# The one-hot products of the gate matrix in f32r, with the gate weight in two parts

## Chip, core and metric

The kernel runs on one NeuronCore of a Trainium2 chip. The metric is the device time of one execution in microseconds (us). One execution was also recorded by the hardware profiler; times inside the kernel come from that record. Engines are named as the profile names them: PE is the matrix engine's products, PEld its weight loads, DVE the vector engine, ACT the scalar engine, POOL the GpSimd engine, SP the queue that issues most transfers.

## What is computed

Two transformer-like blocks over 256 tokens of width 2048. The change touches the last part of the second block, the retrieval over 16384 experts (`peer`): each token has 8 heads with 16 chosen experts, each with a weight g, and an expert is a pair of keys (i1, i2) out of 128 by 128.

```python
sc, pos = lax.top_k(cand, PEER_TOPK)
idx = jnp.take_along_axis(cand_idx, pos, axis=-1)      # i1 * 128 + i2
g = jax.nn.softmax(sc, axis=-1)
act = jax.nn.gelu(jnp.einsum('thkd,td->thk', u[ib], tb), approximate=False)
return jnp.einsum('thk,thkd->td', gb * act, v[ib])
```

The kernel doesn't gather rows of u and v. It multiplies all experts by all tokens, and weighs the result with a gate matrix that holds, for each token, the 128 by 128 table of summed weights (zero for an expert that was not chosen).

## The kernel before

All weights come as one stream of 128-column blocks, each 1 MB (`raw`). ACT casts each half of a block to f32r (`whi`, L337) and DVE subtracts that from the raw values to get the remainder (`wlo`, L343). PE then makes three f32r products in place of one fp32 product (high by high, high by low, low by high). f32r is a second 4-byte format of PE, into which the high part is rounded.

The stage of the change is the up-projection: 128 blocks, one for 128 experts (`product_wide`, L375 and L376). Per block there are 16 pairs of f32r products: one of 512 columns (high weights by both parts of the activations) and one of 256 columns. Block n's result is copied and added by ACT (L1775) and DVE (`usum`, L1508), and DVE prepares the remainders of block n + 2. Every engine runs a fixed program in order; semaphores tie them together. The loops over `n` in the code give the order.

The gate matrix is made beside this stage, in 64 groups of 4 tokens. `groups_at(n)` spreads them over n = 58 to 113: one group per block, and two in each seventh or so. The parts are:

- routing on DVE up to block 54, then the three tables of chosen key 1, key 2 and weight are turned by PE so that the 128 chosen entries lie on the partitions, and copied to `chosenT` (L1464);
- for group g, at DVE's step n (after `usum`), one instruction makes four one-hot tables of key 2 (`one2`, L1471, 128 by 512), and four instructions make the one-hot table of key 1 times the weight (`one1`, L1477, 128 by 128 each);
- at PE's step n + 2, after the block's products, `gate_group` (L963) multiplies the two tables for each of the 4 tokens: weights `one2`, moving operand `one1`, 128 columns, fp32;
- ACT copies the bank to `gstage` (L1757), and POOL's queue stores it.

The tables have four buffers each; DVE's group g waits for PE's group g - 4. PE's group waits for `onehots` and for ACT's copy of four groups before. The down-projection (L994 to L996) follows: per block 24 f32r products of 512 columns.

Of the kernel before, what the change touches and what calls it, by code (L numbers as in the profile page):

```python
# [13 lines left out]
T = 256  # L14
# [133 lines left out]
def build(nc, stream, xt, vecs, sgu_wt, sgu_b, relb, buckets, keys, inv_cnt, lnf, out):  # L148
    f32, f32r, u32 = mybir.dt.float32, mybir.dt.float32r, mybir.dt.uint32
    ALU, ACT, AX = mybir.AluOpType, mybir.ActivationFunctionType, mybir.AxisListType  # L150
# [7 lines left out]
    def at(name, shape, offset, dtype=f32):  # L158
        return nc.alloc_sbuf_tensor_at(name, shape, dtype, offset=int(offset))

    def ar(name, shape, kb, dtype=f32):

        return at(name, shape, ARENA + kb * KB, dtype)
# [5 lines left out]
    iota = at("iota", [128, 128], origin + 3 * KB)  # L169
# [96 lines left out]
    chosen = [ar(f"chosen{i}", [128, KC, TOPK], 26 + i) for i in range(3)]  # L266
    gsum = ar("gsum", [128, KC], 106)
    chosenT = [ar(f"chosenT{i}", [128, T], 29 + i) for i in range(3)]
    one1 = [ar(f"one1_{i}", [128, 4, 128], 16 + 2 * i) for i in range(4)]
    one2 = [ar(f"one2_{i}", [128, 4, 128], 96 + 2 * i) for i in range(4)]  # L270
    gstage = [ar(f"gstage{i}", [128, SLICES, 32, 16], 64 - 16 * i) for i in range(2)]
    gslice = [ar(f"gslice{i}", [128, T, 16], 48 + 16 * i) for i in range(2)]

# [12 lines left out]
    def bank(i):  # L286
        return pb[i]

    es = ExitStack()
    with es:  # L290
# [3 lines left out]
        def sem(name):  # L294
            if name not in made:
                made[name] = es.enter_context(nc.semaphore(name))
            return made[name]

        def vcol(name, i=0, p0=0, p1=128):
            return vec[p0:p1, VCOL[name] + i:VCOL[name] + i + 1]  # L300
# [418 lines left out]
        def _(pe):  # L719
            pe.wait_ge(sem("onehot_loaded"), 32)  # L720
            nc.tensor.matmul(bank(7)[0:16, 0:128], relb_sb[:, :], onehot_b[:, :], start=True,
                             stop=True).then_inc(sem("band_product"), 1)
# [9 lines left out]
            for j in range(NT):  # L732
                ins = nc.tensor.transpose(bank(4 + 3 * j)[:, 0:128], ckv[:, 1, 128 * j:128 * j + 128], ident[:, :])
# [32 lines left out]
            for r in range(4):  # L766
                for h in range(2):
                    for j in range(NT):
                        ins = nc.tensor.transpose(bank(4 + r)[:, 256 * h + 128 * j:256 * h + 128 * j + 128],
                                                  bv[:, 2 * r + h, 128 * j:128 * j + 128], ident[:, :])  # L770
# [3 lines left out]
            for r in range(4):  # L774
                pe.wait_ge(sem("vtok_ready"), r + 1)
                for h in range(2):
                    for j in range(NT):
                        hh = 2 * r + h
                        ins = nc.tensor.matmul(bank(4 + r)[:, 256 * h + 128 * j:256 * h + 128 * j + 128],
                                               vtok[:, j, 128 * hh:128 * hh + 128], sguw[:, hh, :],  # L780
                                               start=True, stop=True)
# [6 lines left out]
            for i in range(WC):  # L788

                o = bank(4 + i // 2)[:, T * (i % 2):T * (i % 2) + T]  # L790
                for k in range(2):
# [3 lines left out]
                    ins = nc.tensor.matmul(o, wlo[b.half][:, w, :], mixhi[:, r, :], start=False, stop=k == 1)  # L795
# [39 lines left out]
            for i, src in enumerate((cum, dtfs)):  # L835
                for j in range(NT):
                    ins = nc.tensor.transpose(bank(6)[:, 256 * i + 128 * j:256 * i + 128 * j + 128],
                                              src[:, 128 * j:128 * j + 128], ident[:, :])
# [15 lines left out]
            for g in range(2):  # L854
                B, C, o = xconv[:, 8 + g, :], xconv[:, 10 + g, :], bank(4 + g)
                nc.tensor.matmul(o[:, 0:256], B[:, 0:128], C, start=True, stop=True)
                nc.tensor.matmul(o[:, 256:384], B[:, 128:256], C[:, 128:256], start=True,
                                 stop=True).then_inc(sem("cb_product"), 1)
# [10 lines left out]
            for h in range(HEADS):  # L869
                if h % 2 == 0:  # L870
                    beside_ssd(3 + h // 2, 4 + h // 2)
                if h >= 2:
                    pe.wait_ge(sem("ssd_out"), h - 1)
                pe.wait_ge(sem("ssd_mat"), h + 1)
                c, m, o = h // 2, dec[h % 2], bank(6 + h % 2)
                nc.tensor.matmul(o[:, 0:256], xtok[:, 0, 128 * c:128 * c + 128], m[:, 0:256], start=True, stop=False)
                nc.tensor.matmul(o[:, 128:256], xtok[:, 1, 128 * c:128 * c + 128], m[:, 256:384], start=False,
                                 stop=True).then_inc(sem("ssd_y"), 1)
# [46 lines left out]
            for n in range(8):  # L925
# [3 lines left out]
                for i in range(4):  # L929
                    hs = 4 * q + i  # L930
                    ins = nc.tensor.matmul(bank(4 + n % 4)[:, 128 * i:128 * i + 128], pq[:, hs, 128 * j:128 * j + 128],
                                           pk[:, hs, :], start=True, stop=True)
# [24 lines left out]
            def gate_group(g):  # L957

                pe.wait_ge(sem("onehots"), g + 1)
                if g >= 4:  # L960
                    pe.wait_ge(sem("stage_full"), g - 3)
                for t in range(4):
                    ins = nc.tensor.matmul(bank(4 + g % 4)[:, 128 * t:128 * t + 128], one2[g % 4][:, t, :],  # L963
                                           one1[g % 4][:, t, :], start=True, stop=True)
                ins.then_inc(sem("gate_product"), 1)

            for n in range(CHUNKS):
# [41 lines left out]
        def _(dve):  # L1009
            st = Steps(dve, sem("dve_steps"))  # L1010
# [100 lines left out]
            for r in range(4):  # L1111
                dve.wait_ge(sem("b_spatial"), r + 1)
                t = bsq[:, 2 * r:2 * r + 2, :]
                for h in range(2):
                    bias_h = sgub[:, 2 * r + h, :].rearrange("p (a n) -> p a n", a=1).to_broadcast([128, NT, 128])
                    ins = nc.vector.tensor_tensor(bsq[:, 2 * r + h, :].rearrange("p (j n) -> p j n", j=NT),
                                                  bank(4 + r)[:, T * h:T * h + T].rearrange("p (j n) -> p j n", j=NT),
                                                  bias_h, ALU.add)
# [18 lines left out]
            for g, src in enumerate((win_a[:, 0:2, PAD:], win_b[:, 0:2, PAD:], win_a[:, 4:6, PAD:],  # L1137
                                     win_b[:, 4:6, PAD:])):
                by = cnt[:, g, :].rearrange("p (a n) -> p a n", a=1).to_broadcast([128, 2, T])
                ins = nc.vector.tensor_tensor(src, src, by, ALU.mult)  # L1140
# [58 lines left out]
            for q in range(4):  # L1199
                part = zsum[:, 4 * q:4 * q + 4, :]  # L1200
# [6 lines left out]
            for c in range(KC):  # L1207
                dve.wait_ge(sem("x1_scaled"), c + 1)
                ins = nc.vector.tensor_scalar(x1[:, c, :], zsum[:, c, :], vcol("ln_b", c), None, ALU.add)
# [19 lines left out]
            def rms_split(name, src, r, gain, n, dhi, dlo, tmp, j0=0, c0=0):  # L1229

                for c in range(n):
# [11 lines left out]
            ins = nc.vector.tensor_scalar(y[:, :], bank(b.bank)[:, 0:T], vcol("dtf_bias"), vcol("dtf_sign"), ALU.add,  # L1243
                                          ALU.mult)
# [47 lines left out]
            for r in range(4):  # L1292
                dve.wait_ge(sem("xs_turned"), r + 1)
                for h in range(2):
                    c = 2 * r + h
                    ins = nc.vector.tensor_tensor(
                        xtok[:, :, 128 * c:128 * c + 128].rearrange("p j (a d) -> p j a d", a=2),
                        bank(4 + r)[:, 256 * h:256 * h + 256].rearrange("p (j a d) -> p j a d", j=NT, a=2),
                        dtT[:, :, 2 * c:2 * c + 2].rearrange("p j (a d) -> p j a d", d=1).to_broadcast([128, NT, 2, 64]),
                        ALU.mult)  # L1300
# [159 lines left out]
            def turned_chosen():  # L1460

                dve.wait_ge(sem("chosen_turned"), 1)
                for i in range(3):
                    st.link(nc.vector.tensor_copy(chosenT[i][:, :], bank(4 + i)[:, 0:T]))  # L1464

            def onehots(g):

                o = g % 4
                if g >= 4:
                    dve.wait_ge(sem("gate_product"), g - 3)  # L1470
                nc.vector.tensor_tensor(  # L1471
                    one2[o][:, :, :], iota[:, :].rearrange("p (a n) -> p a n", a=1).to_broadcast([128, 4, 128]),
                    chosenT[1][:, 4 * g:4 * g + 4].rearrange("p (a n) -> p a n", n=1).to_broadcast([128, 4, 128]),
                    ALU.is_equal)
                for t in range(4):
                    tok = slice(4 * g + t, 4 * g + t + 1)
                    ins = nc.vector.tensor_scalar(one1[o][:, t, :], iota[:, :], chosenT[0][:, tok],  # L1477
                                                  chosenT[2][:, tok], ALU.is_equal, ALU.mult)
                ins.then_inc(sem("onehots"), 1)

            def gate(j):
# [49 lines left out]
            for t in range(NT):  # L1531
                for q in range(4):
                    dve.wait_ge(sem("rows_done"), 4 * t + q + 1)
                    part = x1tok[:, t, 512 * q:512 * q + 512]
# [12 lines left out]
                for q in range(4):  # L1547
                    part = x1tok[:, t, 512 * q:512 * q + 512]
# [350 lines left out]
```

## Time and profile before

| what | value |
|---|---|
| median of 3 runs | 3460.86 us (3460.77 to 3461.58) |
| the profiled execution, its own time | 3458.67 us |
| span from its first to its last instruction | 3456.9 us |
| PE busy | 3286.3 us, 95% of the span |
| DVE busy | 2072.9 us, 60% |
| ACT busy | 1516.0 us, 44% |
| chain that ended last | PE 89%, DVE 6%, ACT 2% |
| L963, the one-hot products, in that chain | 1% |

The page divides the span by engine and by line of the code. PE's busy time there has modelled ends, and its products overlap, so the pace of PE is read from the distance between starts and not from a product's own duration. The chain that ended last tells which instructions the end of the kernel depended on.

### The profile page before, as it was taken

The numbers are of one execution on the slowest core, as the hardware profiler recorded it, in microseconds if no ns is written. First come the engines' busy times: TensorE is split into PE (matmuls) and PEld (weight loads), VectorE is DVE, ScalarE is ACT, GpSimd is POOL, SyncE is SP. The second block draws the span as 40 slices with busy tenths as digits, with TensorE's granted clock in tenths as the row PEclk, the third lists the DMA queues.
The fourth block names the chain that finished last, engine by engine and source line by source line (L and its number), as shares of the span: only waits on it lengthen the run. The fifth ranks groups of instructions, "written<-read, shape, count | busy, mean of one in ns | idle before, by whom it ended". The sixth has DMA issues, their size and how long they took to land.

```text
span 3456.9 us, 54474 instructions
## 1 busy us (share of the span) xinstructions
PE 3286.3 (95%) x21910; PEld 3041.9 (88%) x21910; DVE 2072.9 (60%) x3174; ACT 1516.0 (44%) x2095; POOL 29.1 (1%) x44
## 2 busy tenths in 40 slices
PE   7989998999999997999888999999999999999998
PEld 7878998999999997999778988888888888888886
DVE  4446977555545446675335478967676566666665
ACT  4444434444444334434224444454444444444444
POOL 0000000000000000000000000000000000000000
PEclk9989999999999998999889999999999999999999
DMA  9323543555555542434123466656666866666663
GB/s 282 125 96 138 186 163 134 177 182 182 182 182 182 194 171 83 173 126 155 61 85 135 160 206 207 210 201 228 221 215 230 310 244 243 242 240 241 240 219 139
DMA packets 108255, 638.72 MB, mean 185 GB/s; under 512 B 11616, under 2 KB 28160, under 8 KB 38960
## 3 DMA queue, kind: packets, MB, share of 16 engines
q1 hardware_dynamic: 100368, 591.44, 48.3%
q0 software_dynamic: 7472, 44.57, 3.6%
q8 instruction: 125, 2.05, 0.2%
q14 instruction: 50, 0.41, 0.0%
q10 hardware_dynamic: 240, 0.25, 0.0%
HBM read 597.42 MB, written 38.80 MB: 184 GB/s over the span
## 4 chain that ended last, share of the span: by engine, by line
PE 89%; DVE 6%; ACT 2%; issue 1%; DMA 1%; DVEq 0%; ACTq 0%; SPq 0%
PE bank L375 14%; PE bank L358 14%; PE bank L360 14%; PE bank L359 14%; PE bank L376 7%; PE bank L994 7%; PE bank L995 7%; PE bank L996 7%; DVE wlo L343 2%; PE bank L963 2%; PE bank L497 1%; ACT whi L337 1%; PE bank L494 1%; DMA raw<-stream 1%; PE bank L508 1%
## 5 line engine op out<-in xcount | busy, mean ns | idle before, releaser
L343 DVE TENSOR_TENSOR wlo<-raw,whi 128x1024 fp32r<-128x1024 f32 x1056 | 1288.6, 1225 | 1208.5 <-ACT whi L337 1205.5
L337 ACT CAST whi<-raw 128x1024 fp32r<-128x1024 f32 x1056 | 1104.5, 1048 | 1308.8 <-PE bank L360 783.8
L358 PE MATMUL bank<-xboth,whi 128*128 128x256 f32 x3312 | 948.9, 287 | 39.9 <-DVE xboth L1225 24.1
L359 PE MATMUL bank<-xboth,whi 128*128 128x256 f32 x3312 | 942.0, 284 | 0.0
L360 PE MATMUL bank<-xboth,wlo 128*128 128x256 f32 x3312 | 941.8, 284 | 0.0
L375 PE MATMUL bank<-xboth,whi 128*128 128x512 f32 x2048 | 727.0, 399 | 0.0
L358 PEld LDWEIGHTS bank<-xboth,whi 128*128 128x128 f32 x3312 | 641.6, 194 | 42.7 <-issue 39.7
L359 PEld LDWEIGHTS bank<-xboth,whi 128*128 128x128 f32 x3312 | 641.1, 194 | 0.7
L360 PEld LDWEIGHTS bank<-xboth,wlo 128*128 128x128 f32 x3312 | 640.7, 193 | 0.0
L376 PE MATMUL bank<-xboth,wlo 128*128 128x256 f32 x2048 | 573.1, 280 | 0.0
L375 PEld LDWEIGHTS bank<-xboth,whi 128*128 128x128 f32 x2048 | 384.7, 188 | 89.8
L994 PE MATMUL bank<-whi,aghi 128*128 128x512 f32 x1024 | 398.4, 389 | 0.0
L996 PE MATMUL bank<-wlo,aghi 128*128 128x512 f32 x1024 | 398.3, 389 | 0.0
L995 PE MATMUL bank<-whi,aglo 128*128 128x512 f32 x1024 | 398.3, 389 | 0.0
L376 PEld LDWEIGHTS bank<-xboth,wlo 128*128 128x128 f32 x2048 | 386.6, 189 | 0.0
L996 PEld LDWEIGHTS bank<-wlo,aghi 128*128 128x128 f32 x1024 | 192.3, 188 | 39.9
L994 PEld LDWEIGHTS bank<-whi,aghi 128*128 128x128 f32 x1024 | 192.3, 188 | 39.9
L995 PEld LDWEIGHTS bank<-whi,aglo 128*128 128x128 f32 x1024 | 192.3, 188 | 39.8
L1767 ACT CAST aghi<-agf 128x256 fp32r<-128x256 f32 x128 | 52.1, 407 | 272.5 <-DVE agf L1491 272.5
L358 PE MATMUL bank<-mhi,whi 128*128 128x256 f32 x512 | 151.5, 296 | 12.0 <-DVE mlo L1360 6.8
L359 PE MATMUL bank<-mlo,whi 128*128 128x256 f32 x512 | 147.0, 287 | 0.0
L360 PE MATMUL bank<-mhi,wlo 128*128 128x256 f32 x512 | 147.0, 287 | 0.0
(348 smaller groups left out, 3030.8 us busy)
## 6 DMA issues: line engine op xcount, KB each, us to landing
raw<-stream SPq DMA_DIRECT2D x528, 1024.0 KB, 4.8
up_activations<-ust SPq DMA_DIRECT2D x128, 128.0 KB, 5.1
gate_matrix<-gstage POOLq DMA_DIRECT2D x8, 2048.0 KB, 14.0
gslice<-gate_matrix POOLq DMA_DIRECT2D x8, 2048.0 KB, 10.7
uin<-up_activations SPq DMA_DIRECT2D x32, 512.0 KB, 5.6
relative_band<-cband POOLq DMA_DIRECT2D x1, 3072.0 KB, 36.8
xraw<-xt SPq DMA_DIRECT2D x1, 2048.0 KB, 7.8
cbias<-relative_band POOLq DMA_DIRECT2D x1, 2048.0 KB, 20.8
```

The source lines that it names most:

```text
L337: nc.scalar.copy(whi[b.half][:, k, :], raw[b.raw][:, k, :]).then_inc(hi_done, 1)
L343: nc.vector.tensor_tensor(wlo[b.half][:, k, :], raw[b.raw][:, k, :], whi[b.half][:, k, :].bitcast(f32), ALU.subtract).then_inc(lo_done, 1)
L358: nc.tensor.matmul(o, whi[b.half][:, k, :], rhi[:, r, :], start=i == 0, stop=False)
L359: nc.tensor.matmul(o, whi[b.half][:, k, :], rlo[:, r, :], start=False, stop=False)
L360: ins = nc.tensor.matmul(o, wlo[b.half][:, k, :], rhi[:, r, :], start=False, stop=i == len(ks) - 1)
L375: nc.tensor.matmul(o[:, :], whi[b.half][:, k, :], xboth[:, :, k, :], start=k == 0, stop=False)
L376: ins = nc.tensor.matmul(o[:, 0:T], wlo[b.half][:, k, :], xhi[:, k, :], start=False, stop=k == KC - 1)
L963: ins = nc.tensor.matmul(bank(4 + g % 4)[:, 128 * t:128 * t + 128], one2[g % 4][:, t, :], one1[g % 4][:, t, :], start=True, stop=True)
L994: nc.tensor.matmul(o[:, :], a_hi[:, tok], v_hi[:, col], start=j == 0, stop=False)
L995: nc.tensor.matmul(o[:, :], a_lo[:, tok], v_hi[:, col], start=False, stop=False)
L996: ins = nc.tensor.matmul(o[:, :], a_hi[:, tok], v_lo[:, col], start=False, stop=j == CHUNKS - 1)
L1767: nc.scalar.copy(aghi[j % 3][:, :], agf[j % 3][:, :]).then_inc(sem("ag_hi"), 1)
```

## The change

The weight's column is split once into an f32r part and the remainder (two DVE instructions of 128 by 256). Each one-hot table of key 1 is made twice, times the one and times the other part, both in f32r; the table of key 2 is written in f32r as well. Each fp32 product becomes two f32r products that add into the same place.

```diff
-    one1 = [ar(f"one1_{i}", [128, 4, 128], 16 + 2 * i) for i in range(4)]
-    one2 = [ar(f"one2_{i}", [128, 4, 128], 96 + 2 * i) for i in range(4)]
+    one1 = [[ar(f"one1_{part}{i}", [128, 4, 128], at_kb + 2 * i, f32r) for i in range(4)]
+            for part, at_kb in (("hi", 16), ("lo", 8))]
+    one2 = [ar(f"one2_{i}", [128, 4, 128], 96 + 2 * i, f32r) for i in range(4)]
+    wgt_hi = ar("wgt_hi", [128, T], 104, f32r)
+    wgt_lo = ar("wgt_lo", [128, T], 105)
...
                 for t in range(4):
-                    ins = nc.tensor.matmul(bank(4 + g % 4)[:, 128 * t:128 * t + 128], one2[g % 4][:, t, :],
-                                           one1[g % 4][:, t, :], start=True, stop=True)
+                    for part in range(2):
+                        ins = nc.tensor.matmul(bank(4 + g % 4)[:, 128 * t:128 * t + 128], one2[g % 4][:, t, :],
+                                               one1[part][g % 4][:, t, :], start=part == 0, stop=part == 1)
...
                     st.link(nc.vector.tensor_copy(chosenT[i][:, :], bank(4 + i)[:, 0:T]))
+                st.link(nc.vector.tensor_copy(wgt_hi[:, :], chosenT[2][:, :]))
+                st.link(nc.vector.tensor_tensor(wgt_lo[:, :], chosenT[2][:, :], wgt_hi[:, :].bitcast(f32),
+                                                ALU.subtract))
...
                 for t in range(4):
                     tok = slice(4 * g + t, 4 * g + t + 1)
-                    ins = nc.vector.tensor_scalar(one1[o][:, t, :], iota[:, :], chosenT[0][:, tok],
-                                                  chosenT[2][:, tok], ALU.is_equal, ALU.mult)
+                    for part, weight in enumerate((wgt_hi[:, :].bitcast(f32), wgt_lo)):
+                        ins = nc.vector.tensor_scalar(one1[part][o][:, t, :], iota[:, :], chosenT[0][:, tok],
+                                                      weight[:, tok], ALU.is_equal, ALU.mult)
```

On PE, at the end of the first block with groups (n = 60), this stood between the block's last products and the next block's first; an fp32 product is one row here, `x4` stands for four in a row:

```order
L375 MATMUL bank<-xboth,whi_57 128x512
L376 MATMUL bank<-xboth,wlo_59 128x256
L963 MATMUL bank<-one_0_182,one_0_186 128x128 x4
L963 MATMUL bank<-one_1_183,one_1_187 128x128 x4
L375 MATMUL bank<-xboth,whi_58 128x512
L376 MATMUL bank<-xboth,wlo_60 128x256
```

In the changed program the first of the two groups begins so; eight rows of L967 make a group, the high and the low table in turn (three lines of code were added above, so L375 is L378, L376 is L379 and L963 is L967; `one_hi` and `one_lo` are the two tables of key 1, `one_0` that of key 2):

```order
L378 MATMUL bank<-xboth,whi_57 128x512
L379 MATMUL bank<-xboth,wlo_59 128x256
L967 MATMUL bank<-one_hi_182,one_0_190 128x128
L967 MATMUL bank<-one_lo_186,one_0_190 128x128
L967 MATMUL bank<-one_hi_182,one_0_190 128x128
```

Each product of a group has become a product with the high and one with the low table, at the same place between the blocks.

On DVE, at n = 58, the work of two groups stood before the remainders of the next block:

```order
L1508 TENSOR_TENSOR usum_197<-bank,upart_195 128x256
L1471 TENSOR_TENSOR one_0_186<-iota,chosenT_180 128x512
L1477 TENSOR_SCALAR one_0_182<-iota,chosenT_179,chosenT_181 128x128 x4
L1471 TENSOR_TENSOR one_1_187<-iota,chosenT_180 128x512
L1477 TENSOR_SCALAR one_1_183<-iota,chosenT_179,chosenT_181 128x128 x4
L343 TENSOR_TENSOR wlo_60<-raw_54,whi_58 128x1024 x2
```

In the changed program (L343 is L346, L1508 is L1516, L1471 is L1478, L1477 is L1485) the first of the two groups begins so, with eight rows of L1485:

```order
L1516 TENSOR_TENSOR usum_203<-bank,upart_201 128x256
L1478 TENSOR_TENSOR one_0_190<-iota,chosenT_180 128x512
L1485 TENSOR_SCALAR one_hi_182<-iota,chosenT_179,wgt_hi 128x128
L1485 TENSOR_SCALAR one_lo_186<-iota,chosenT_179,wgt_lo 128x128
L1485 TENSOR_SCALAR one_hi_182<-iota,chosenT_179,wgt_hi 128x128
```

The second group ends so, and the next block's remainders follow:

```order
L1485 TENSOR_SCALAR one_hi_183<-iota,chosenT_179,wgt_hi 128x128
L1485 TENSOR_SCALAR one_lo_187<-iota,chosenT_179,wgt_lo 128x128
L346 TENSOR_TENSOR wlo_60<-raw_54,whi_58 128x1024 x2
L1516 TENSOR_TENSOR usum_204<-bank,upart_202 128x256
L1478 TENSOR_TENSOR one_2_192<-iota,chosenT_180 128x512
```

Four instructions of 128 by 128 per group have become eight, all of them ahead of the next remainders; the table of key 2 is still one instruction. Once, after the copies to `chosenT`, a cast to `wgt_hi` and a subtraction to `wgt_lo` have been added. Nothing else moves on any engine.

## Rows read from the trace of the kernel before

**Rows 1.** the page: the chain that ended last, share of the span by engine

```profile
PE 89%; DVE 6%; ACT 2%; issue 1%; DMA 1%; DVEq 0%; ACTq 0%; SPq 0%
```

**Rows 2.** the chain from 2300 to 2700 us: shares, then pieces (start us, us)

```profile
by line: PE bank L375 56.9%; PE bank L376 28.9%; PE bank L963 14.3%
...
2329.57 0.89 PE bank L963 x8
2336.01 0.89 PE bank L963 x8
2342.55 0.89 PE bank L963 x8
```

**Rows 3.** timeline of PE and PEld at two groups (start us, us, engine, line)

```profile
2500.37 1.87 PEld L963 LDWEIGHTS bank<-one,one 128*128 128x128 f32 x16
2500.49 1.95 PE L963 MATMUL bank<-one,one 128*128 128x128 f32 x16
...
2502.16 0.19 PEld L375 LDWEIGHTS bank<-xboth,whi 128*128 128x128 f32 x1
```

**Rows 4.** single lines, duration ns minimum/median/maximum: fp32 128, fp32 256, f32r 256 columns

```profile
L931 PE MATMUL bank<-pk,pq x64: 275/275/348, 1959.3 to 1966.4; 128*128 128x128 f32 x64
...
L409 PE MATMUL bank<-zsum,ones x32: 377/378/483, 1209.1 to 1292.7; 128*128 128x256 f32 x32
...
L358 PE MATMUL bank<-yhi,whi x512: 283/283/283, 654.2 to 1183.7; 128*128 128x256 f32 x171
```

**Rows 5.** timeline of the weight loads where f32r products start after idle time

```profile
642.53 0.19 PEld L358 LDWEIGHTS bank<-xboth,whi 128*128 128x128 f32 x1 [0.84 <-DVE wlo L343]
642.64 0.19 PEld L359 LDWEIGHTS bank<-xboth,whi 128*128 128x128 f32 x1
642.76 0.19 PEld L360 LDWEIGHTS bank<-xboth,wlo 128*128 128x128 f32 x1
```

**Rows 6.** timeline of PE in the down-projection, f32r products of 512 columns

```profile
3000.02 0.39 PE L994 MATMUL bank<-whi,aghi 128*128 128x512 f32 x1
...
3000.70 0.39 PE L994 MATMUL bank<-whi,aghi 128*128 128x512 f32 x1
```

**Rows 7.** timeline of PE in the up-projection, twice the first and last of 19 L375

```profile
2099.69 0.40 PE L375 MATMUL bank<-xboth,whi 128*128 128x512 f32 x1
...
2106.05 0.40 PE L375 MATMUL bank<-xboth,whi 128*128 128x512 f32 x1
...
2709.95 0.40 PE L375 MATMUL bank<-xboth,whi 128*128 128x512 f32 x1
...
2716.19 0.40 PE L375 MATMUL bank<-xboth,whi 128*128 128x512 f32 x1
```

**Rows 8.** DVE groups by line and form: count, busy us, mean ns

```profile
L1477 DVE TENSOR_SCALAR one<-iota,chosenT,chosenT 128x128 f32<-128x128 f32 x256 | 71.1, 342 | 0.0
...
L551 DVE TENSOR_SCALAR fprob<-fprob,fsmall 128x256 f32<-128x256 f32 x16 | 5.6, 348 | 0.0
...
L550 DVE TENSOR_SCALAR fprob<-fprob,fsmall 128x128 f32<-128x128 f32 x16 | 4.6, 286 | 0.6
```

**Rows 9.** timeline of DVE at a step with two groups, to the next remainders

```profile
2489.92 0.42 DVE L1508 TENSOR_TENSOR usum<-bank,upart 128x256 f32<-128x256 f32 x1
2490.25 0.69 DVE L1471 TENSOR_TENSOR one<-iota,chosenT 128x512 f32<-128x512 f32 x1
2490.85 1.11 DVE L1477 TENSOR_SCALAR one<-iota,chosenT,chosenT 128x128 f32<-128x128 f32 x4
2491.88 0.69 DVE L1471 TENSOR_TENSOR one<-iota,chosenT 128x512 f32<-128x512 f32 x1
...
2493.50 1.22 DVE L343 TENSOR_TENSOR wlo<-raw,whi 128x1024 fp32r<-128x1024 f32 x1
2495.22 1.23 DVE L343 TENSOR_TENSOR wlo<-raw,whi 128x1024 fp32r<-128x1024 f32 x1 [0.50 <-ACT whi L337]
```

**Rows 10.** one window: busy of PE, PEld, DVE, ACT, POOL, granted clock, DMA share

```profile
2315.00:2680.00 365.00, 365.00 (x2277) 326.25 (x2277) 252.48 (x471) 178.84 (x284) 6.25 (x7) 1.00 0.65 222
```

## The prediction

> **What bounds the kernel now.** I read the chain that ended last first: PE holds 89% of the span [rows 1]. Then the same chain in the stretch of the change: between 2300 and 2700 us it is only PE, 56.9% L375, 28.9% L376 and 14.3% L963, the one-hot products [rows 2]. So every nanosecond of L963 is a nanosecond of the kernel, and nothing that DVE, ACT or a transfer does there is late. PE is busy all 365.00 us of the window from 2315 to 2680 at a granted clock of 1.00, the 2.4 GHz level; DVE is busy 252.48 us of it [rows 10].
>
> What L963 costs comes from starts, since the durations overlap. One fp32 product is recorded as two weight loads and two products. Over two groups, sixteen records, the first weight load starts at 2500.37 and that of the next block's first product at 2502.16: 1.79 / 16 = 112 ns for each [rows 3]. The chain gives the same: 0.89 us for eight [rows 2]. All 64 groups are 512 records, 57.3 us, and 28.7 us would go if two f32r products cost half of one fp32 product.
>
> **PE: 256 fp32 products out, 512 f32r products in.** Before, there are two records for each fp32 product and each takes 112 ns; after, there are 512 f32r products with a record and a weight load each. The number of records stays at 512, so all depends on what an f32r product of 128 columns costs against 112 ns. The trace has no f32r product under 256 columns, so I bound it.
>
> By columns alone it would be cheap. fp32 products last 275 ns with 128 columns and 378 with 256: 103 ns for 128 columns, two PE cycles a column. f32r products last 283 ns with 256 columns [rows 4] and start 120 ns apart (642.64 to 642.76, which is spacing of weight loads and products alike [rows 5]), and those of 512 columns start 227 ns apart (0.68 us for three [rows 6]). That is 107 ns for 256 columns, one cycle a column, and a fixed 13. For 128 columns: 53 + 13 = 67 ns.
>
> But each product first needs its weights, and the next load begins only when the product before has begun. How long a load takes shows where PE has been idle: the first f32r load starts at 642.53 and the second at 642.64, 0.11 us later, though no product stood in the way of the first [rows 5]. The second load can only begin when the first weights have moved on, so an f32r load of 128 weights takes about 108 ns, against 67 ns of product. Under 256 columns the load is the longer of the two. The Trainium skill says so too: TensorE: Matmul & The Clock Gate, section LDWEIGHTS, has the load take P / 1.2 ns, 107 ns for 128 columns, whatever the contraction; by that the products would cost 512 x (107 - 112) = 2.6 us less than before.
>
> So the lower bound of the mechanism is 108 ns: 512 x (108 - 112) = -2.0 us. The upper one is the pace of f32r products of 256 columns, 120 ns, if the 13 ns come on top of the load: 512 x (120 - 112) = +4.1 us. I take 110, near the load, because the fp32 records that have the same load run at 112 with 107 ns of columns: 512 x (110 - 112) = **-1.0 us**.
>
> **PE: the pace of the wide products.** One pair of L375 and L376 took 6.36 / 18 = 353 ns at 2100 us and 6.24 / 18 = 347 ns at 2710 us, at the same clock and with nothing else in between [rows 7]. The groups toggle it: they follow each other 6.44 us apart and then 6.54 [rows 2], so a block differs by 0.10 us. I count two quick blocks to one slow among the 55 with groups, 37 and 18 (an estimate: the rows show one of each), and the 12 behind them as quick [rows 7]. I can't say from the rows which pace follows an f32r group. All quick would be -1.8 us, all slow 49 x 0.10 = +4.9 us. I take no change.
>
> **DVE: 256 more instructions.** L1477 lasts 342 ns, but the next starts earlier: the four and the table of key 2 take 1.63 us (2490.25 to 2491.88), the four from 2490.85 take 1.03, so 257 ns each [rows 9]. Each group gets 4 x 0.257 = 1.03 us more, 66 us in all. At one group a step this falls into idle time: DVE's load is (252.48 + 61 x 1.03) / 365 = 86% with the 61 groups of the window [rows 10]. At a step with two groups it is 2.06 us: the remainders that began at 2493.50 begin at 2495.56, the next at 2496.8 instead of 2495.22 [rows 9]. Behind them wait `usum` and the next tables, and PE for the remainders. PE reads those of 2493.50 when it starts the block behind its own two groups, at 2502.16 [rows 3], 7.4 us after they were ready (1.22 us from 2493.50). A delay of 2.1 us stays hidden and is worked off in the two steps that follow. The tables themselves are used two steps later, from 2500.37, and would be ready at 2495.56. The raw blocks are reloaded 2 us later at most, against a ring of four. What hides all of it is PE; if PE's load went away, DVE's 86% would be the next bound.
>
> The two instructions of the weight's split run once, under a microsecond, at a step without groups: hidden. ACT, POOL and the queues do the same as before.
>
> **The sum.** 3456.9 us of span, -1.0 for the records, 0 for pace and DVE: 3455.9. The profiled execution took 3458.67 us with 3456.9 of span, and the median of the runs is 2.2 above it; the change applied to the median is 3460.86 - 1.0 = 3459.9 us. The ends of this case: 3460.86 - 2.0 - 1.8 = 3457.1 and 3460.86 + 4.1 + 4.9 = 3469.9.
>
> **Rivals.**
>
> (a) The f32r product of 128 columns isn't one quick pass. Only 256 and 512 columns are seen at one cycle a column. If below that PE treats it as it treats an fp32 product, each of the 512 costs two records, 224 ns: 512 x 112 ns = +57.3 us, 3518 us. For it: every product of 128 columns in the trace runs at two cycles a column. Against: those are all fp32, and fp32 of 256 columns does too [rows 4], so it goes with the format and not with the number of columns.
>
> (b) The load doesn't bound. If the load could begin before the product ahead of it, 67 ns would stand: 512 x (67 - 112) = -23.0 us, 3437.8 us. Against: the spacing of 0.11 us of loads behind an idle PE [rows 5]. The Trainium skill (TensorE: Matmul & The Clock Gate, section Back-to-back issue gap) goes this way: it has pairs of load and product at 128 columns sustain about 81 ns. By it the sum would be 512 x (81 - 112) = -15.9 us; nothing in this trace runs at that pace, and all weights here are 4-byte.
>
> (c) DVE becomes the bound. It has 365 us for 61 groups; full load comes at (365 - 252.48) / 61 = 1.84 us more per group, so at (1.84 + 1.03) / 8 = 359 ns for each of the eight instructions, against 257 now. An f32r output at half the element rate would add 62 ns (348 ns for 256 elements, 286 for 128 [rows 8]) and give 319: still below. It decides only if the instructions stop overlapping and their duration grows as well, to 342 + 62 = 404 ns: 64 x 8 x 45 ns = 23 us, less the 7.4 us that PE has in hand, +16 us, 3476 us.
>
> (d) The change doesn't do what it says: PE would need fewer records than 512 for a gain. That is (b) by another way, for instance if the second product of a pair kept its weights. L358 and L359 have the same weights one after the other, and each has its own load [rows 5]: no such saving is made.
>
> **How the numbers follow.** About 0.2%, 6.9 us, is what a measurement of this kernel can tell from no change: 3453.9 to 3467.8. The load-bound case has a chance of 0.77, of which 0.04 lie above 3467.8 (slow records and the slow pace together). (a) 0.15, (b) and (d) 0.05, (c) 0.03. Faster 0.05, same 0.73, slower 0.15 + 0.03 + 0.04 = 0.22. The range takes the whole first case and (c) and leaves (a) and (b) out, 0.20 together: 3455 to 3477.
>
> **What would show it.** In the changed trace the product line has 512 records again. From the first load of a group to the next block's first load divided by eight is 108 to 120 ns if I am right, 67 if (b), 224 (or 1024 records) if (a). The chain between 2300 and 2700 us is still PE alone; a wait of PE for `wlo` or the tables there would be (c). The four instructions that are now eight keep a distance near 257 ns. The periods of 6.44 and 6.54 us show the pace. What would make me wrong without any of this: a change of pace beyond both of those seen, since the rows give its size but no reason.

## The result: slower by 4.8 us, all of it in the pace of the wide products

The changed kernel takes 3465.55 us (median of 20 runs), the kernel before 3460.77 us beside it: 4.8 us more, a ratio of 1.0014 with a 95% interval of 1.0007 to 1.002. The forecast was 3459.9 us. The measured time lies inside the range of 3455 to 3477 and under the 0.2% that were called no change, but it moved the other way.

The first place to look is where the time is. The two rows are the products of 512 columns of the up-projection, before and changed: duration in ns (minimum, median, maximum), then the start of the first and of the last of them.

```profile
L375 PE MATMUL bank<-xboth,whi x2048: 391/395/481, 1966.4 to 2746.0; 128*128 128x512 f32 x187
L378 PE MATMUL bank<-xboth,whi x2048: 393/398/481, 1968.5 to 2753.0; 128*128 128x512 f32 x187
```

The stage took 779.6 us before and takes 784.5 us now, 4.9 us more. The profiled executions differ by 7.1 us (3456.9 and 3464.0 us of span): the other 2.1 us lie ahead of the stage, where the two programs do the same. The stage starts at 1966.4 to 1970.8 us in the profiled executions of this study.

PE still holds the chain, with 89% of the span as in [rows 1]. Between 2300 and 2700 us the chain is again PE alone, as in [rows 2], and the one-hot products (now L967) have a smaller share of it, 13.6% against 14.3%. The pieces are those of the groups (start in us, length):

```profile
by line: PE bank L378 57.7%; PE bank L379 28.8%; PE bank L967 13.6%
...
2344.85 0.84 PE bank L967 x8
2351.39 0.84 PE bank L967 x8
2357.93 0.84 PE bank L967 x8
```

Before, the groups followed each other 6.44 us apart and then 6.54 [rows 2]. Here it is 6.54 and 6.54. The blocks behind the last group differ too. The next two rows are PE's timeline of the changed kernel, the first and the seventeenth of its products of 512 columns, so 16 pairs:

```profile
2709.91 0.40 PE L378 MATMUL bank<-xboth,whi 128*128 128x512 f32 x1
...
2715.57 0.40 PE L378 MATMUL bank<-xboth,whi 128*128 128x512 f32 x1
```

5.66 us for 16 pairs, 353 ns a pair, where [rows 7] had 347 ns in the same place. So all blocks now run at the slow pace. What hardly changed is the price of the group. These are the weight loads of one group and of the next block's first product in the changed kernel:

```profile
2491.20 0.19 PEld L967 LDWEIGHTS bank<-one_hi,one 128*128 128x128 f32 x1
2491.32 0.19 PEld L967 LDWEIGHTS bank<-one_lo,one 128*128 128x128 f32 x1
...
2492.10 0.19 PEld L378 LDWEIGHTS bank<-xboth,whi 128*128 128x128 f32 x1
```

From 2491.20 to 2492.10 there are eight loads, 0.90 / 8 = 112 ns each, the same as with fp32 in [rows 3]. The group's piece of the chain is 0.84 us where it was 0.89, because the second product of a group now starts 0.06 us behind the first (2491.32 and 2491.38) and not 0.11; the loads don't come closer for it.

And DVE, in the window of [rows 10], is busy 313.06 us in place of 252.48, with nobody waiting for it. PE has no wait in that window; DVE's own wait for ACT has shrunk from 111.2 to 51.9 us. The first row is the kernel before, the others are the changed one:

```profile
L343 DVE TENSOR_TENSOR wlo<-raw,whi 128x1024 fp32r<-128x1024 f32 x111 | 136.0, 1225 | 111.2 <-ACT whi L337 111.2
...
2315.00:2680.00 365.00, 365.00 (x2254) 324.09 (x2253) 313.06 (x725) 177.49 (x283) 6.25 (x7) 1.00 0.63 219
...
L346 DVE TENSOR_TENSOR wlo<-raw,whi 128x1024 fp32r<-128x1024 f32 x112 | 135.4, 1220 | 51.9 <-ACT whi L340 51.9
L1485 DVE TENSOR_SCALAR one_hi<-iota,chosenT,wgt_hi 128x128 fp32r<-128x128 f32 x248 | 84.3, 340 | 0.0
L1485 DVE TENSOR_SCALAR one_lo<-iota,chosenT,wgt_lo 128x128 fp32r<-128x128 f32 x248 | 84.2, 340 | 0.0
```

The starts of all blocks in the trace of the kernel before give the number of quick ones: 36 of the 55 between the first and the last group, and the 12 behind them. In the changed kernel none is quick. 48 blocks at 0.10 us each are 4.8 us, and the medians differ by 4.8.

### The profile page after: what moved, and what is told of

It reads as the page before. It is cut to its first block, busy times and chain, and to the rows that moved or that the text cites. A ratio compares the mean times of both kernels' runs of the same rounds, so it can differ in the third digit from the quotient of the medians.

```text
span 3464.0 us, 54732 instructions
## 1 busy us (share of the span) xinstructions
PE 3291.9 (95%) x21910; PEld 3043.9 (88%) x21910; DVE 2134.4 (62%) x3432; ACT 1515.8 (44%) x2095; POOL 29.3 (1%) x44
## 4 chain that ended last, share of the span: by engine, by line
PE 89%; DVE 6%; ACT 2%; issue 1%; DMA 1%; DVEq 0%; ACTq 0%; SPq 0%
PE bank L378 14%; PE bank L361 14%; PE bank L363 14%; PE bank L362 14%; PE bank L379 7%; PE bank L998 7%; PE bank L999 7%; PE bank L1000 7%; DVE wlo L346 2%; PE bank L967 2%; PE bank L500 1%; ACT whi L340 1%; PE bank L497 1%; DMA raw<-stream 1%; PE bank L511 1%
## 5 line engine op out<-in xcount | busy, mean ns | idle before, releaser
L346 DVE TENSOR_TENSOR wlo<-raw,whi 128x1024 fp32r<-128x1024 f32 x1056 | 1286.6, 1224 | 1151.8 <-ACT whi L340 1148.8
L378 PE MATMUL bank<-xboth,whi 128*128 128x512 f32 x2048 | 730.2, 400 | 0.0
L379 PE MATMUL bank<-xboth,wlo 128*128 128x256 f32 x2048 | 575.2, 281 | 0.0
L378 PEld LDWEIGHTS bank<-xboth,whi 128*128 128x128 f32 x2048 | 385.1, 188 | 92.7
L379 PEld LDWEIGHTS bank<-xboth,wlo 128*128 128x128 f32 x2048 | 387.1, 189 | 0.0
```

The costliest lines, as they stand in the source:

```text
L346: nc.vector.tensor_tensor(wlo[b.half][:, k, :], raw[b.raw][:, k, :], whi[b.half][:, k, :].bitcast(f32), ALU.subtract).then_inc(lo_done, 1)
L378: nc.tensor.matmul(o[:, :], whi[b.half][:, k, :], xboth[:, :, k, :], start=k == 0, stop=False)
L379: ins = nc.tensor.matmul(o[:, 0:T], wlo[b.half][:, k, :], xhi[:, k, :], start=False, stop=k == KC - 1)
```

## The experiments

Times are medians; each stands beside runs of the kernel before on the same chip (3460.1 to 3460.8 us in all of them). "Quick" and "slow" are the two paces of a pair of wide products, 347 and 353 ns.

### DVE's part of the change alone

```diff
+    one1lo = [ar(f"one1_lo{i}", [128, 4, 128], 8 + 2 * i, f32r) for i in range(4)]
...
+                    nc.vector.tensor_scalar(one1lo[o][:, t, :], iota[:, :], chosenT[0][:, tok],
+                                            chosenT[2][:, tok], ALU.is_equal, ALU.mult)
                     ins = nc.vector.tensor_scalar(one1[o][:, t, :], iota[:, :], chosenT[0][:, tok],
```

> The kernel before with DVE's part of the change alone: for each token a second, unused table of key 1 in f32r, so eight instructions per group in place of four; PE keeps its fp32 products. Theory P (what PE runs between the blocks sets the pace of the wide products, and DVE has nothing to do with it): time of before within 1 us, two thirds of the blocks with groups at 347 ns a pair, one third at 353, the blocks behind at 347. Rival D (the longer DVE work beside the wide products slows their reading): about 4.8 us above before, all pairs at 353 ns.

Measured: 3460.1 us against 3460.63, ratio 0.9998 (0.9988 to 1.0007). The rows are the chain at three groups, then the busy time of the window; L964 is the one-hot product here:

```profile
2332.05 0.89 PE bank L964 x8
2338.49 0.89 PE bank L964 x8
...
2345.04 0.89 PE bank L964 x8
...
2315.00:2680.00 365.00, 365.00 (x2275) 326.12 (x2275) 314.55 (x727) 178.97 (x284) 6.25 (x7) 1.00 0.64 220
```

6.44 and 6.55: the pattern of before, with DVE busy 314.55 us of 365. From the first product behind the first groups to the first behind the last group, 56 blocks on, the traces of this run and of the kernel before both have 368.10 us. DVE's work is hidden in full and doesn't touch the pace. Theory D falls. What remains is on PE.

### What an f32r product of few columns costs

```diff
-                        ins = nc.tensor.matmul(bank(4 + g % 4)[:, 128 * t:128 * t + 128], one2[g % 4][:, t, :],
-                                               one1[part][g % 4][:, t, :], start=part == 0, stop=part == 1)
+                        ins = nc.tensor.matmul(bank(4 + g % 4)[:, 128 * t:128 * t + 64], one2[g % 4][:, t, :],
+                                               one1[part][g % 4][:, t, 0:64], start=part == 0, stop=part == 1)
```

> The changed kernel with each one-hot product cut to its first 64 of 128 columns; it leaves out half of the gate matrix. Theory L (the weight load bounds a product of few columns): the eight of a group still start 112 ns apart, eight in 0.84 to 0.90 us of the chain. Rival C (the columns bound, at two cycles each): 54 ns fewer each, 58 ns apart, 27 us less in all.

Measured: 3461.78 us, one run. The weight loads of a group, then the chain at three groups:

```profile
2489.83 0.19 PEld L967 LDWEIGHTS bank<-one_hi,one 128*128 128x128 f32 x1
...
2490.61 0.19 PEld L967 LDWEIGHTS bank<-one_lo,one 128*128 128x128 f32 x1
...
2331.51 0.81 PE bank L967 x8
2338.05 0.81 PE bank L967 x8
...
2344.50 0.81 PE bank L967 x8
```

Eight loads take (2490.61 - 2489.83) / 7 = 111 ns each with half the columns. The load is the floor, as the prediction had it: the 27 us of theory C are not there. The spacing of the groups, 6.54 and 6.45, shows something that was not asked: the pace turns again. These groups are f32r throughout, as in the changed kernel, and have the same loads; only the columns differ. So f32r in the group is not by itself what keeps blocks slow.

### The high tables alone on PE

```diff
-                    for part in range(2):
-                        ins = nc.tensor.matmul(bank(4 + g % 4)[:, 128 * t:128 * t + 128], one2[g % 4][:, t, :],
-                                               one1[part][g % 4][:, t, :], start=part == 0, stop=part == 1)
+                    ins = nc.tensor.matmul(bank(4 + g % 4)[:, 128 * t:128 * t + 128], one2[g % 4][:, t, :],
+                                           one1[0][g % 4][:, t, :], start=True, stop=True)
```

> The changed kernel with PE multiplying the high tables alone; it leaves out the weight's low part, DVE still makes it. 256 records and loads of 112 ns fewer. Theory L and P: 28.7 us less for the records, and the slow pace stays (24 us below before, 28.7 below the changed kernel) or toggles (29 us below before). Rival (the time of the changed kernel comes from DVE's longer work): less than 20 us below the changed kernel.

Measured: 3434.64 us against 3460.48, ratio 0.9925 (0.991 to 0.994): 25.8 us below before, and 30.9 below the changed kernel, which was measured separately. The chain at three groups:

```profile
2336.10 0.39 PE bank L966 x4
...
2342.09 0.39 PE bank L966 x4
2348.18 0.39 PE bank L966 x4
```

The four products of a group are 0.39 us of the chain and the groups follow at 5.99 and 6.09 us: quick and slow blocks again. 256 loads at 112 ns are 28.7 us; the other 2.2 fit the 24 blocks that are quick in its trace, at 0.10 us each. Load and pace add up.

### Which product of the group matters: one fp32 product last, or first

```diff
+                    o = bank(4 + g % 4)[:, 128 * t:128 * t + 128]
+                    if t == 3:
+                        ins = nc.tensor.matmul(o, one2f[g % 4][:, :], one1f[g % 4][:, :], start=True, stop=True)
+                        continue
```

> The changed kernel with the fourth token of each group as one fp32 product, the last in the group (tables of its own in fp32, still eight small DVE instructions for key 1 and 2 together). Eight records per group as before. Theory P1 (the product right in front of a block sets the pace): the pattern of before comes back, two quick blocks to one slow, and the blocks behind are quick: the time of before within 1 us. Rival P2 (any f32r products of 128 columns in the group, or the phase in which the group is entered, keep it slow): 4.8 us above before.

The other kernel has `t == 0` in the same place.

> The same with the first token of each group as the fp32 product, f32r products last. Theory P1: slow pace after every group, 4.8 us above before. If the way into the group decides instead (the first product right behind the wide ones), the pattern and time of before.

Measured: 3465.2 us with the fp32 product last (ratio 1.0016, 1.0006 to 1.0025) and 3465.4 us with it first (1.0014, 1.0004 to 1.0024). The chain at three groups with the fp32 product last, then at two with it first; L973 is f32r, L970 fp32:

```profile
2331.15 0.62 PE bank L973 x6
2331.76 0.28 PE bank L970 x2
2337.69 0.62 PE bank L973 x6
...
2344.24 0.62 PE bank L973 x6
...
2333.30 0.62 PE bank L973 x6
...
2339.84 0.62 PE bank L973 x6
```

6.54 and 6.55 us in the first, 6.54 in the second. Both are as slow as the changed kernel, so neither the product right ahead of a block nor the one right behind it decides by its format. Theory P1 falls. What I had left was that the pace is a state, which the whole way through a group leaves or turns.

### Four or eight products thrown in where there are no groups

Blocks 8 to 56 are slow in both kernels. Here products that nobody uses were put behind blocks 12, 25 and 38 of the kernel before:

```diff
+                if n in (12, 25, 38):
+                    pe.wait_ge(sem("x1tok_out"), 8)
+                    for t in range(4):
+                        nc.tensor.matmul(bank(4)[:, 128 * t:128 * t + 128], ident[:, :], ident[:, :], start=True,
+                                         stop=True)
```

> The kernel before with four fp32 products of 128 columns into a bank that is free, after blocks 12, 25 and 38, where all blocks run slow (353 ns a pair); the products are not used. They cost 0.89 us each time. Theory S (the pace is a state that the way through a group sets and that then stays): after at least one of the three places the blocks turn to 347 ns and stay there up to the next place, 12 or 13 blocks of 5.55 us. Rival (quick blocks need something of the groups' stretch, such as ACT's and DVE's work on them): all stay at 353.

The f32r form:

```diff
+                    for t in range(8):
+                        nc.tensor.matmul(bank(4)[:, 128 * (t // 2):128 * (t // 2) + 128], xhi[:, t, 0:128],
+                                         xhi[:, t, 0:128], start=t % 2 == 0, stop=t % 2 == 1)
```

> The same with eight f32r products of 128 columns in place of the four fp32 ones, at the same three places, at the same 0.89 us. Theory S with the difference between the kernels coming from the kind of product: all blocks stay at 353 ns. If the kind doesn't matter: the same turns as with the fp32 products.

Measured, one run each: 3459.83 us with the fp32 products, 3463.41 us with the f32r ones. First the fp32 kernel: the chain's piece of the first thrown-in products, then 16 pairs behind the first place (2099.76 to 2105.30) and 16 behind the third (2239.73 to 2245.38):

```profile
2044.94 0.89 PE bank L974 x8
...
2099.76 0.39 PE L375 MATMUL bank<-xboth,whi 128*128 128x512 f32 x1
...
2105.30 0.39 PE L375 MATMUL bank<-xboth,whi 128*128 128x512 f32 x1
...
2239.73 0.40 PE L375 MATMUL bank<-xboth,whi 128*128 128x512 f32 x1
...
2245.38 0.40 PE L375 MATMUL bank<-xboth,whi 128*128 128x512 f32 x1
```

5.54 us behind the first, 5.65 behind the third. Four products of 0.89 us turned 26 blocks to the quick pace, the second place left them quick, and the third turned them back. That is the order slow, quick, quick, slow that the groups of the kernel before go through.

The two quick stretches are not the same. The rows are the products of 512 columns in three windows of this run, behind the first, the second and the third place, with their shortest, median and longest duration in ns:

```profile
L375 PE MATMUL bank<-xboth,whi x88: 392/394/395, 2065.8 to 2095.9; 128*128 128x512 f32 x88
...
L375 PE MATMUL bank<-xboth,whi x88: 391/391/391, 2139.8 to 2170.0; 128*128 128x512 f32 x88
...
L375 PE MATMUL bank<-xboth,whi x86: 395/398/403, 2214.6 to 2244.7; 128*128 128x512 f32 x86
```

The starts say it more clearly: behind the first place the pairs take 343 and 350 ns in turn, behind the second 346, 347, 347, behind the third 349, 350, 361, over and over. So there are three repeating patterns, two of 347 ns a pair and one of 353. The groups of the kernel before lead from each to the next in a fixed turn (slow, first quick, second quick, slow), 18 times over; a block's pattern depends on the pattern ahead of the group and not on the group alone.

Now the f32r kernel, 16 pairs behind the first place and 16 behind the second:

```profile
2099.84 0.39 PE L375 MATMUL bank<-xboth,whi 128*128 128x512 f32 x1
...
2105.39 0.39 PE L375 MATMUL bank<-xboth,whi 128*128 128x512 f32 x1
...
2149.83 0.40 PE L375 MATMUL bank<-xboth,whi 128*128 128x512 f32 x1
...
2155.47 0.40 PE L375 MATMUL bank<-xboth,whi 128*128 128x512 f32 x1
```

5.55 and then 5.64 us: the first turned to quick, the second back to slow, and behind the third they stayed slow. So f32r products can turn the pace as well. In the fp32 kernel the quick blocks gave back 26 x 0.10 = 2.6 us for the 3 x 0.89 = 2.7 us that the thrown-in products took, so its time is that of the kernel before; in the f32r kernel 13 blocks gave back 1.3 us there.

The f32r kernel has two more differences further on, where its program is that of the kernel before. The four blocks ahead of its first groups are quick, and its twelve blocks behind the last group are slow, where those of before are the other way round. The groups' products were fp32 in both; what differed is the pattern in which the stream came to them.

Theory S fits: the pace is a state of the stream of pairs. In these traces it lasts as long as nothing interrupts the stream, whatever ACT and DVE do beside it, and a handful of other products may turn it either way.

### Another order of the wide products

If the state belongs to the strict alternation of 512 and 256 columns, another order has none. Two of a kind together:

```diff
-                nc.tensor.matmul(o[:, :], whi[b.half][:, k, :], xboth[:, :, k, :], start=k == 0, stop=False)
-                ins = nc.tensor.matmul(o[:, 0:T], wlo[b.half][:, k, :], xhi[:, k, :], start=False, stop=k == KC - 1)
+                for step in ((low, wide) if k % 2 else (wide, low)):
+                    ins = step()
```

`wide` is the product of 512 columns and `low` that of 256.

> The kernel before with the order of the wide block's products changed: 512, 256, then 256, 512 columns and so on in turn, so that two of a kind follow each other; the same products. Theory P (the slow pace comes from the strict alternation of 512 and 256 columns, since streams of 512 or of 256 alone always run at columns plus 13 ns): all pairs at 347 ns; the 60 blocks ahead of the groups gain 0.10 us each, the 18 slow ones among them too: 8 us below before. Rival (alternation isn't the cause): no change within 1 us, or all blocks slow, 5 us above.

> The changed kernel with the same order of the wide products as in the run with that order on the kernel before. Theory P: all 128 blocks at 347 ns a pair, the same time as that run within 1 us, so that the 4.8 us of the change are gone. Rival: the changed kernel stays 4.8 us above the other with this order.

Measured: 3456.1 us on the kernel before (ratio 0.9986, 0.9977 to 0.9995) and 3454.95 us on the changed one (0.9985, 0.9976 to 0.9994). PE's timeline of the first (L376 is 512 columns, L380 is 256), then the chain at its groups (L969), then at those of the changed kernel (L973):

```profile
2099.66 0.63 PE L376 MATMUL bank<-xboth,whi 128*128 128x512 f32 x2
...
2100.36 0.63 PE L376 MATMUL bank<-xboth,whi 128*128 128x512 f32 x2
...
2101.75 0.63 PE L376 MATMUL bank<-xboth,whi 128*128 128x512 f32 x2
...
2332.83 0.89 PE bank L969 x8
2339.31 0.89 PE bank L969 x8
...
2345.79 0.89 PE bank L969 x8
...
2332.35 0.84 PE bank L973 x8
...
2338.82 0.84 PE bank L973 x8
...
2345.29 0.84 PE bank L973 x8
```

Four products every 0.70 us (2.09 / 6 = 348 ns a pair), and groups 6.48 us apart, all alike. With this order the change is no longer slower: 3454.95 against 3456.1. The traces place about half of these 1.1 us: the groups of the changed kernel follow each other 6.47 us apart and not 6.48, 0.6 us less over the 56 blocks (367.73 and 368.31 us); the rest isn't settled. The 4.8 us are gone, and the two kernels are 4.4 and 5.5 us faster than the kernel before beside them. The first kernel's gain was half of the 8 us expected: all blocks are alike, but at 348 and not 347 ns, so the blocks that were quick lost a little.

Runs of eight have still fewer changes of width:

```diff
+                for k in ks:
+                    nc.tensor.matmul(o[:, :], whi[b.half][:, k, :], xboth[:, :, k, :], start=k == 0, stop=False)
+                for k in ks:
+                    ins = nc.tensor.matmul(o[:, 0:T], wlo[b.half][:, k, :], xhi[:, k, :], start=False,
```

> The kernel before with the wide block's products in runs of eight: per half block eight of 512 columns, then eight of 256. Theory P (switching between the two widths costs, in either pace): the block takes 16 x (227 + 120) ns = 5.55 us in all 128 blocks, 0.03 us a block under the order in turn by twos (5.573) and 0.10 under the slow pace: 60 x 0.10 + 19 x 0.10 = 8 us below before, 3.5 below that run. Rival (the order in twos was already all that is to be had): equal to that run.

Measured: 3456.99 us (ratio 0.9991, 0.9982 to 1.0). The timeline, where one row is a run of eight (L376 of 512 columns, L378 of 256):

```profile
2102.28 2.00 PE L376 MATMUL bank<-xboth,whi 128*128 128x512 f32 x8
2104.12 1.12 PE L378 MATMUL bank<-xboth,wlo 128*128 128x256 f32 x8
2105.07 2.00 PE L376 MATMUL bank<-xboth,whi 128*128 128x512 f32 x8
```

A half block takes 2.79 us, a block 5.58, where 8 x 0.227 + 8 x 0.120 = 2.77 was expected for a half. No better than the order by twos, and the interval reaches to no change. That each change of width costs something is not borne out. What the two new orders share is that every block clear of other products has one pace; that the strict alternation makes the slow pattern possible is the simplest reading of the three orders, and no run shows how.

### Both together

The high tables alone, as above, with the wide products in runs of eight. The first lines of the edit:

```diff
                 for t in range(4):
-                    for part in range(2):
+                    ins = nc.tensor.matmul(bank(4 + g % 4)[:, 128 * t:128 * t + 128], one2[g % 4][:, t, :],
```

> The same order of the wide products, with the changed kernel's high tables alone in the one-hot products; it leaves out the low part of the weight. Theory L and P, additive: 28.7 us for 256 loads and 8 us for the pace below before: 3424 us. Rival (DVE, with its 315 us of work in the stretch of now about 335, or the loads of the blocks become the bound there): PE waits for wlo or for a table, and the time is above 3428 us.

Measured: 3429.48 us (ratio 0.9909, 0.9894 to 0.9925), above the 3424 us expected by about as much as the order fell short (5.5 and 5 us). It is also above the 3428 us of the rival, but the rival's waits are not there: PE waits for nothing between 2300 and 2700 us. Then with the order by twos:

> The wide block's products in turn by twos (512, 256, 256, 512), which gave the shortest blocks so far (5.573 us against 5.587 in runs of eight), with the changed kernel's high tables alone in the one-hot products; it leaves out the low part of the weight. If load and pace add up: 102 blocks at 5.65 and 24 at 5.55 in the run with the high tables alone become 5.573 each, 102 x 0.077 - 24 x 0.026 = 7.2 us less than its 3434.6: 3427.4 us. Rival (with less work on PE, DVE's tables or the remainders come late): above 3431 us, with waits of PE for wlo.

Measured: 3427.37 us against 3460.46 (ratio 0.9905, 0.9889 to 0.9922), where 3427.4 was expected. DVE is close to being the bound:

```profile
2315.00:2640.00 325.00, 325.00 (x1953) 287.01 (x1952) 304.81 (x710) 172.37 (x274) 6.26 (x7) 1.00 0.70 241
```

It is busy 304.81 us of 325, 94%, and PE still waits for nothing. It makes the low tables for nothing there; a kernel that is content with the high part would leave them out. With the whole of the weight computed, the fastest kernel of the study is the one with the changed products and the order by twos, 3454.95 us.

## The prediction, step by step

- **PE bounds this stretch, and nothing else does**: right. The chain is PE alone in every kernel of the study, with DVE at up to 94%.
- **The weight load is the floor of an f32r product of 128 columns**: right, and it is why halving the passes gave nothing. 112 ns against the 110 taken; 111 ns with 64 columns. The term of -1.0 us came out between 0 and -0.6: the spacing of the loads gives nothing, and where both kernels have one pace, in the order by twos, the 56 blocks with groups take 0.6 us less. Rivals (a), 224 ns, and (b), 67 ns, are excluded by the same rows, and (d) by the count: the changed trace has 2 x 256 loads at L967. The Trainium skill's figure of 81 ns (TensorE: Matmul & The Clock Gate, section Back-to-back issue gap) doesn't hold for these 4-byte weights, which took 112. The same page's P / 1.2 for the load (section LDWEIGHTS), 107 ns, is 5 ns under the spacing measured.
- **DVE's 256 instructions are hidden**: right. 66 us were forecast; the window shows 60.6 more (313.06 - 252.48), against 61 x 1.03 = 62.8, and alone they cost nothing. Rival (c) is excluded, since the eight instructions still start 257 ns apart and last 340 ns.
- **The pace: "I take no change"**: this is the step that failed, and it carries the whole difference. It was a term put at nothing. Its size was right: the end with all blocks slow, +4.9 us, is what was measured (4.8). Its value of zero had no ground. The rows showed that groups turn the pace; to forecast no change was to forecast that other products would turn it just as often. With ends of -1.8 and +4.9 and no reason for either, the middle, +1.5, would at least have had the sign. The count that it rested on was one off: 36 quick and 19 slow blocks and not 37 and 18. That the measured time lies inside the stated range is owed to the width of these ends and of rival (c), not to the value of the sum.

What was not foreseen is that the state could be locked: in the changed kernel all 56 blocks with groups are entered slow and left slow. What in a group sets the state stays open. It is not DVE's work, nor the format of the first or the last product, nor the number of loads alone: eight turn it in the kernel before and not in the changed one, whose loads take the same 0.89 to 0.90 us. The groups of 64 columns and the products thrown in show that the same kind of group may turn it or not. The moment at which the stream starts again, to a few ns, may decide, but no run varied that moment alone. It isn't simply how long the first pair behind the group takes: in the run with f32r products thrown in, a first pair of 403 ns stands ahead of quick blocks at the first place and of slow ones at the third.

## To carry to other kernels

In a stream of products of 128 columns in a 4-byte format, each with 128 fresh weights, the products come no closer than the loads, here every 112 ns; splitting an fp32 product into two f32r products keeps the number of loads and gains next to nothing. A gain needs fewer loads. One product in place of two gave 28.7 us here; more columns for each load, at the same work, should do so too, which no run tried. Where a stream alternates between two widths of product, measure its pace over whole blocks and try another order of the same products, before a difference of 0.1% is put down to an edit next to it.

## What the runs showed of the hardware that I had not expected

- The same pairs of products, 512 and 256 columns, at the same granted clock (1.00, the 2.4 GHz level) and with nothing else on PE, run at 347 or at 353 ns a pair, and keep to it for dozens of blocks until other products come between. There are three patterns of distances between pairs: 343 and 350 ns, or 346, 347, 347, or 349, 350, 361.
- Four unused products, 0.89 us, turned the following 13 blocks from 5.65 to 5.55 us each.
- The order 512, 256, 256, 512 has one pace, 348 ns a pair, in every block that stands clear of other products; runs of eight have 2.79 / 8 = 349 ns.
- In a stream with a load each, f32r products of 64 columns come no closer than those of 128, 111 and 112 ns.
- On DVE an f32r output costs a small `tensor_scalar` nothing: 340 ns for 128 elements, 342 with an fp32 output [rows 8].
